# Two token tiles, one after the other in the last two weight chunks: a two-block transformer kernel on one core

## What is computed

```python
def second_block(x, ...):
    for layer in range(DEPTH):                       # two layers
        if layer % 2 == 0:
            y = even_mixer(x, ...)                   # its last product is ev_out
        else:
            y = odd_mixer(x, ...)                    # its last product is od_out
        x = layer_norm(ALPHA * x + y, ln1_g[layer], ln1_b[layer])
        f = conv_ffn(x, ...)                         # fup0/fup1 up, fdown0/fdown1 down
        x = layer_norm(ALPHA * x + f, ln2_g[layer], ln2_b[layer])
    return x

def layer_norm(x, g, b):
    mu = x.mean(-1, keepdims=True)
    var = jnp.square(x - mu).mean(-1, keepdims=True)
    return (x - mu) * lax.rsqrt(var + LN_EPS) * g + b
```

## Time and profile before

| | us |
|---|---|
| median of three runs | 1284.06 |
| the three runs | 1279.86, 1292.66, 1284.06 |
| span of the profiled execution | 1289.9 |

### The profile page before, as it was taken

How to read it: one execution, slowest core, us unless ns; L and a number is a source line. 1 busy time by engine, 2 the same in 40 slices (tenths; PEclk the granted TensorE clock), 3 DMA queues, 4 the chain that set the end, 5 groups by cost and what they waited for, 6 DMA issues and landing times.

```text
span 1289.9 us, 22283 instructions
## 1 busy us (share of the span) xinstructions
PE 1226.5 (95%) x8846; PEld 1143.1 (89%) x8846; DVE 536.4 (42%) x948; ACT 671.7 (52%) x920; POOL 957.2 (74%) x750
## 2 busy tenths in 40 slices
PE   4899999999989999999999998999998898999997
PEld 4788999999968999999987778999887776999985
DVE  4866331110485242110543745744204646464502
ACT  5366555443665555343544346666536555565541
POOL 5856679979843879889695346998895844898893
PEclk9799999999989999999999798999998998999999
DMA  6563345554431445545553124464453432555451
GB/s 260 196 181 103 131 160 208 189 187 169 173 121 38 163 160 200 195 162 196 196 176 126 66 96 157 173 229 170 180 205 131 164 131 99 180 212 195 168 193 33
DMA packets 33140, 208.69 MB, mean 162 GB/s; under 512 B 3432, under 2 KB 7656, under 8 KB 8472
## 3 DMA queue, kind: packets, MB, share of 16 engines
q1 hardware_dynamic: 29728, 199.22, 43.1%
q10 hardware_dynamic: 3320, 8.14, 2.0%
HBM read 206.29 MB, written 1.59 MB: 161 GB/s over the span
## 4 chain that ended last, share of the span: by engine, by line
POOL 55%; issue 24%; PE 17%; DVE 2%; ACT 1%; DMA 0%; POOLq 0%; DVEq 0%; SPq 0%; ACTq 0%
POOL w_lo L2317 55%; PE bank L284 5%; PE bank L286 5%; PE bank L285 5%; ACT w_hi L1069 0%; DMA raw<-stream 0%; DVE stats L1658 0%; ACT arena L1505 0%; PE bank L1011 0%; ACT h L1167 0%; DVE bank L1672 0%; POOLq L2314 0%; PE bank L1026 0%; DVE arena L2257 0%; DVE stats L1666 0%
## 5 line engine op out<-in xcount | busy, mean ns | idle before, releaser
L2317 POOL TENSOR_TENSOR w_lo<-raw,w_hi 128x512 fp32r<-128x512 f32 x744 | 954.4, 1322 | 312.5 <-ACT w_hi L1069 312.2
L284 PE MATMUL bank<-xs_hi,w_hi 128*128 128x256 f32 x1648 | 477.6, 290 | 23.7 <-POOL w_lo L2317 17.3
L285 PE MATMUL bank<-xs_lo,w_hi 128*128 128x256 f32 x1648 | 473.6, 287 | 0.0
L286 PE MATMUL bank<-xs_hi,w_lo 128*128 128x256 f32 x1648 | 473.3, 287 | 0.0
L1069 ACT ACTIVATE w_hi<-raw 128x2048 fp32r<-128x2048 f32 x186 | 354.5, 1913 | 194.5 <-PE bank L286 159.4
L284 PEld LDWEIGHTS bank<-xs_hi,w_hi 128*128 128x128 f32 x1648 | 324.1, 197 | 30.6 <-issue 30.0
L285 PEld LDWEIGHTS bank<-xs_lo,w_hi 128*128 128x128 f32 x1648 | 324.2, 197 | 0.4 <-issue 0.2
L286 PEld LDWEIGHTS bank<-xs_hi,w_lo 128*128 128x128 f32 x1648 | 323.9, 197 | 0.0
L284 PE MATMUL bank<-hT_hi,w_hi 128*128 128x256 f32 x680 | 194.6, 286 | 2.1 <-issue 1.9
L286 PE MATMUL bank<-hT_hi,w_lo 128*128 128x256 f32 x680 | 192.3, 283 | 0.0
L285 PE MATMUL bank<-hT_lo,w_hi 128*128 128x256 f32 x512 | 144.9, 283 | 0.0
(11 more groups left out here) (312 smaller groups left out, 1409.2 us busy)
## 6 DMA issues: line engine op xcount, KB each, us to landing
raw<-stream SPq DMA_DIRECT2D x186, 1024.0 KB, 4.8
arena<-ln_rows ACTq DMA_DIRECT2D x4, 1024.0 KB, 5.7
arena<-vec_scratch ACTq DMA_DIRECT2D x8, 256.0 KB, 8.7
con<-consts SPq DMA_DIRECT2D x1, 1288.0 KB
h<-x SPq DMA_DIRECT2D x1, 1024.0 KB, 4.9
out<-h SPq DMA_DIRECT2D x4, 256.0 KB, 2.4
con<-pool_mat ACTq DMA_DIRECT2D x1, 768.0 KB, 8.4
vec_scratch<-vec_row ACTq DMA_DIRECT2D x1, 512.0 KB
```

The source lines that it names most:

```text
L284: mm(out, lh, rh, start=start, stop=False, skip_group_check=True)
L285: mm(out, lh, rl, start=False, stop=False, skip_group_check=True)
L286: return mm(out, ll, rh, start=False, stop=stop, skip_group_check=True)
L2317: ins = nc.gpsimd.tensor_tensor(w_lo[:, slot_c].rearrange("p a b -> p (a b)")[:, part], raw[:, slot_r, part], w_hi[:, slot_c].rearrange("p ...
```

## The change

The last two chunks ahead of each norm are used for token tile 0 first and for tile 1 after it. In last_half, chunk c is used for both tiles with k = 0 and 1, for tile 0 with k = 2 and 3, and its last two steps, tile 1 with k = 2 and 3, come behind tile 0's steps of chunk c + 1. In down_by_tokens both last chunks are waited for, then tile 0 takes all eight steps, then tile 1. used_up for the first of the two chunks moves with its last step. VectorE's piece(0, 1) moves behind invert(0) for i = 5 and 7. No operation is added or taken away.

```diff
--- before.py
+++ after.py
@@ -345,19 +345,23 @@
                 c = START[name] + 2
                 hi, lo = half_views(c)
                 o = [claim(pe, (name, 1, t)) for t in range(TT)]
-                for k in range(4):
-                    pe.wait_ge(S("xs_ready"), XS[wait] - 3 + k)
-                    for t in range(TT):
-                        last = by_tokens(o[t], hi, lo, k, src, k, t, start=(k == 0), stop=(k == 3))
-                used_up(last)
+                steps = [(0, 0), (0, 1), (1, 0), (1, 1), (2, 0), (3, 0)]
+                for k, t in steps:
+                    if t == 0:
+                        pe.wait_ge(S("xs_ready"), XS[wait] - 3 + k)
+                    last = by_tokens(o[t], hi, lo, k, src, k, t, start=(k == 0), stop=(k == 3))
+                filled(last, (name, 1, 0))
+                sums()
+                hi2, lo2 = half_views(c + 1)
                 for t in range(TT):
-                    filled_by_chunk((name, 1, t), c)
-                sums()
-                hi, lo = half_views(c + 1)
-                for t in range(TT):
-                    o = claim(pe, (name, 1, 2 + t))
+                    if t == 1:
+                        for k in (2, 3):
+                            last = by_tokens(o[1], hi, lo, k, src, k, 1, start=False, stop=(k == 3))
+                        used_up(last)
+                        filled_by_chunk((name, 1, 1), c)
+                    o2 = claim(pe, (name, 1, 2 + t))
                     for k in range(4):
-                        last = by_tokens(o, hi, lo, k, src, k, t, start=(k == 0), stop=(k == 3))
+                        last = by_tokens(o2, hi2, lo2, k, src, k, t, start=(k == 0), stop=(k == 3))
                     if t == 0:
                         filled(last, (name, 1, 2))
                 used_up(last)
@@ -386,21 +390,34 @@
             def down_by_tokens(name, kt, ready, i):
 
                 chunks, o = 2 * kt // 4, {}
-                for c in range(chunks):
+
+                def step(c, hi, lo, u, t):
+
+                    n, k = divmod(4 * c + u, kt)
+                    key = (name, 2 * n + t)
+                    if n == 0 and t == 0:
+                        pe.wait_ge(S("hidden_ready"), ready + k + 1)
+                    if k == 0:
+                        o[n, t] = claim(pe, key)
+                    last = by_tokens(o[n, t], hi, lo, u, (hT_hi, hT_lo), k, t, start=(k == 0), stop=(k == kt - 1))
+                    if k == kt - 1 and (n, t) != (1, 1):
+                        filled(last, key)
+                    return last
+
+                for c in range(chunks - 2):
                     hi, lo = half_views(START[name] + c)
-                    steps = [(u, t) for u in range(4) for t in range(TT)] if c < chunks - 1 else \
-                        [(u, t) for t in range(TT) for u in range(4)]
-                    for u, t in steps:
-                        n, k = divmod(4 * c + u, kt)
-                        key = (name, 2 * n + t)
-                        if n == 0 and t == 0:
-                            pe.wait_ge(S("hidden_ready"), ready + k + 1)
-                        if k == 0:
-                            o[n, t] = claim(pe, key)
-                        last = by_tokens(o[n, t], hi, lo, u, (hT_hi, hT_lo), k, t, start=(k == 0), stop=(k == kt - 1))
-                        if k == kt - 1 and (n, t) != (1, 1):
-                            filled(last, key)
+                    for u in range(4):
+                        for t in range(TT):
+                            last = step(c, hi, lo, u, t)
                     used_up(last)
+                final = {c: tuple(half_views(START[name] + c)) for c in (chunks - 2, chunks - 1)}
+                for t in range(TT):
+                    for c in final:
+                        hi, lo = final[c]
+                        for u in range(4):
+                            last = step(c, hi, lo, u, t)
+                        if t == 1:
+                            used_up(last)
                 filled_by_chunk((name, 3), START[name] + chunks - 1)
                 if i < 8:
                     turned(i)
@@ -1678,7 +1695,8 @@
                         .then_inc(S("result_dve"), 1)
 
                 piece(0, 0)
-                piece(0, 1)
+                if i in (6, 8):
+                    piece(0, 1)
                 piece(1, 0)
                 if i == 8:
                     dve.wait_ge(S("ln_rows_loaded"), 16 * 4)
@@ -1695,6 +1713,8 @@
                     finished(0, 1)
                     return
                 invert(0)
+                if i in (5, 7):
+                    piece(0, 1)
                 piece(1, 1)
                 invert(1)
                 key = last_piece(i, 1, 1)
```

## The result

| | before | changed |
|---|---|---|
| median of 20 runs each | 1281.31 us | 1286.95 us |
| lowest, highest | 1274.74, 1292.66 | 1281.44, 1295.25 |
| span of the profiled execution | 1289.9 | 1283.9 |
| last matmul ahead of norm 5 to the end of the span | 510.0 | 516.5 |

The ratio changed to before is 1.0054, 95% interval 1.0033 to 1.0074: the change makes the kernel 0.5% slower, 6.9 us (4.2 to 9.5), or 5.6 by the medians. So I compare from the last matmul ahead of norm 5 to the end: 1289.9 - 779.89 = 510.0 and 1283.9 - 767.41 = 516.5.

The account below looks back on a forecast made before the run. TensorE, busy 95% of the span, bounds the long stages; serial chains bound the norms' ends. 2.63 + 1.48 + 0.93 - 0.80 = +4.2 us on the 1284.06 median gave 1288.3 us, range 1280 to 1297.

Parts of the forecast that it names:

- the queue: ScalarE runs in order: its last cut, released 2.72 us later, stands ahead of the norm's table warm-up, square roots and normalisations.
- Norm 5, +2.63: Layer norm after ev_out: tile 1's square root starts 2.63 us later, at 784.88 against 782.25; bounds 2.3 and 3.9.
- Norm 6, +1.48: Layer norm after fdown0: second square root 1.48 us later, from 977.68 to 979.16; bounds 1.05 and 2.7.
- Norm 7, +0.93: Layer norm after od_out: second root 0.93 us later, with the last matmul 0.67 later; bounds 0.4 and 2.2.
- Norm 8, -0.80: Layer norm at the end, no cut left: piece(1, 1) starts 0.80 us earlier; bounds 0 and -0.9.
- The holds: At norms 5, 6 and 7, L1666, with two SBUF inputs, is held to the end of a GpSimd operation.
- rival C: L1666 falls between GpSimd operations at each norm and the restart catches higher clock earlier: 1.0 us slower, 1285; chance 0.14.
- E: Every hold goes the bad way and the clock adds 2: 10.0 us slower, 1294; chance 0.07.
- Rival D: fdown0 and fdown1: TensorE stops, waiting for two chunks at once, up to 5.4 us each; say 1295; chance 0.05.
- Rival B: Tile 0's lead arrives because ScalarE's cut isn't in the way: 3.1 us faster, 1281.0; chance 0.12.
- The table load: Norms 5 and 6: no drain after the load; the skill's 1.4 us drain each would make the sum near 7.
- the clock: TensorE's low granted clock after norms: longer idle could change it by 1.5 us each; taken as nothing, 2 either way.

Follow-up runs that it names:

- e4: The kernel before with only the new last_half, and VectorE's new order in norms 5 and 7 alone; ratio to before 1.0041.
- e9: e1 with tile 1's k = 2 step of od_out moved back ahead of tile 0's k = 3; ratio to the kernel before 0.9989.
- e1: The changed kernel with ScalarE's last cut ahead of norms 5, 6 and 7 put behind the norm; ratio to the kernel before 0.9954.
- e10: e9 with seven idle matmuls of 256 columns added to each of norms 5, 6 and 7; ratio to the kernel before 0.9941.
- e2: The kernel before, old tile order, with ScalarE's last cut put behind the norm; ratio to before 0.9953.
- e8: The changed kernel run and traced once more, unaltered; ratio to the kernel before 1.0072.
- e11: The kernel before run and traced once more, unaltered; ratio 1.0011.
- e3: The kernel before with only the new down_by_tokens (norms 6 and 8), VectorE's order left as it was; ratio to before 1.0006.
- e5: The changed kernel with the square-root table loaded ahead of ScalarE's last cut, the cut still ahead of the norm; ratio to before 1.0038.
- e12: The kernel before with the cut behind the norm, five idle matmuls a norm and the new order in fdown1 alone; ratio to before 0.9932.

## Why the prediction was right, and where it was short

The forecast was 4.2 us slower, for the reason of the queue; measured are 5.6 by the medians and 6.9 by the ratio, whose interval goes from 4.2 to 9.5. That the median itself, 1286.95, lies only 1.35 below the forecast's 1288.3 is luck in part: the median of three runs from which the forecast started was 2.75 above that of twenty, and the change was taken 1.4 too low.

- Norm 5, +2.63: the second root moved from 2.36 to 4.95 us behind the last matmul's end, +2.59. The cut, the table load, the hold of L1666 and the two pieces stood where the working had them. That piece(0, 1) was moved behind the inversion is a part of it, as forecast: tile 0's bank was long there.
- Norm 6, +1.48: the root moved by 1.43 (2.37 to 3.80), the gap by 1.86. The rest, 0.4, is tile 1's transposes at the low clock (1.97 us against 1.15), as in e4; the prediction let them be as fast as before.
- Norm 7, +0.93: 0.27 in the root, plus the hole ahead of it, worked out at 0.67; e9, which fills that hole, measured 0.71.
- Norm 8, -0.80: the tail is 0.87 shorter.
- The holds: L1666 was to end 1.91, 1.91 and 0.62 us behind the last matmul's end of norms 5, 6 and 7, and ended 1.88, 1.88 and 0.65 behind it, each time with the end of one GpSimd operation. Neither rival C, which has it fall between two operations, nor E, which has it wait for one end more, came about.
- The cover taken for the sweep and for the two chunks held: no wait of TensorE for GpSimd appeared at either place. Rival D is out. Rival B, a gain if the queue weren't there, was priced at 3.1 us; e1's rest is 3.0 to 3.8 us below the two traces of before, and its timed ratio is lower still.
- The table load: load and activation follow each other with 0.02 us between them (766.72 + 1.28, then 768.02). By the rule of the Trainium skill, page ScalarE: Activation LUTs, section What ACT_TABLE_LOAD costs, a drain of 1.4 us would lie there. It doesn't here, and the sum of 7 that the rule gave rested on a wait that no row has.
- The term that was short, as far as the runs show it, is the clock, "I take nothing, and 2 us either way". It has a direction. The windows of the gaps and of the 10 us behind them, changed kernel and then the kernel before (columns as in e10, the granted clock third from the end):

```profile
767.41:777.26 9.85, 3.71 (x17) 2.40 (x17) 7.65 (x17) 6.74 (x16) 4.33 (x4) 0.72 0.34 127
777.26:787.26 10.00, 9.99 (x66) 10.00 (x67) 2.72 (x5) 5.31 (x8) 5.03 (x4) 0.77 0.04 7
966.13:974.83 8.70, 3.91 (x16) 2.59 (x17) 6.26 (x15) 6.63 (x16) 4.31 (x4) 0.70 0.43 157
974.83:984.83 10.00, 10.00 (x65) 10.00 (x66) 2.77 (x6) 7.44 (x11) 5.02 (x4) 0.75 0.05 8
1077.57:1086.32 8.75, 3.60 (x17) 2.40 (x17) 7.61 (x16) 5.76 (x13) 4.32 (x4) 0.77 0.34 120
1086.32:1096.32 10.00, 10.00 (x61) 10.00 (x62) 2.10 (x4) 4.76 (x8) 5.01 (x4) 0.69 0.00 1
```

```profile
779.89:787.15 7.26, 3.61 (x16) 2.40 (x17) 5.88 (x14) 5.65 (x13) 1.65 (x2) 0.74 0.51 178
787.15:797.15 10.00, 10.00 (x72) 10.00 (x73) 3.38 (x6) 6.01 (x8) 5.05 (x4) 0.85 0.05 8
975.31:982.16 6.85, 2.79 (x16) 1.67 (x17) 5.77 (x14) 5.70 (x13) 1.64 (x2) 0.94 0.55 207
982.16:992.16 10.00, 10.00 (x61) 10.00 (x62) 2.71 (x5) 7.26 (x11) 5.03 (x4) 0.70 0.06 8
1083.06:1091.54 8.48, 3.61 (x17) 2.40 (x17) 6.95 (x15) 5.81 (x14) 1.63 (x2) 0.74 0.34 124
1091.54:1101.54 10.00, 10.00 (x62) 10.00 (x63) 2.24 (x4) 4.90 (x8) 5.03 (x4) 0.71 0.00 1
```

Low clock is 2 x (1 - clock) x length. For norm 6 of the changed kernel that is 2 x 0.30 x 8.70 + 2 x 0.25 x 10 = 10.2 us; before, 2 x 0.06 x 6.85 + 2 x 0.30 x 10 = 6.8. Over the three norms the record of the granted clock has 30.7 us in both traces of the changed kernel and 23.9 in both of before. In all traces without idle matmuls it has 36 such gaps: of 17 longer than 8.3 us, 15 went with a low period of 10.2 us; of 19 shorter ones, one did, the others with 6.8 or 3.4. (I drew that line afterwards, between the gaps of 7.85 and 8.32; no run looked for a limit.) At norm 7 it was 10.2 in both kernels; what the change lengthened is at norms 5 and 6. Most of the longer period falls into the gap itself, where only the transposes feel it: 0.4 us in norm 6, nothing in norm 5, where they were slow before as well. That is the part of the excess over 4.2 that is shown.

The other 1.0 us of the traces' 5.6 isn't. By the means of two traces each, the stretch behind norm 5 is 0.2 shorter in the changed kernel, that behind norm 6 1.4 longer (0.7 of it from the hole), that behind norm 7 0.6 longer. The low clock in the 10 us behind the restarts is 0.9 us more in the changed kernel (15.8 and 14.0 against 14.9 and 13.2), which costs half of that. But the two traces of before differ by 1.3, 0.5 and 0.9 us in these three stretches themselves, so this may be spread.

What stays open is the timed ratios' own spread: against their traces, e1 and e2 came out some 2 us faster, e9 2 us and e8 4 us slower.

## What to carry to other kernels

An engine's program is a queue. A release that comes later costs whatever stands behind the instruction that waits for it, so when a buffer's last use is moved, look for the prefetch that waits for it and ask what latency-bound work is behind it; here the fix was to put that prefetch behind the norm, and it was worth 0.5%, in the old order too. A tiny vector operation on the critical chain should have one tensor in SBUF and not two, where GpSimd's sweep runs beside it. And look at the granted clock in and behind a gap of TensorE: here the gaps cost again there, and idle matmuls that fitted into TensorE's waits took that away (another 5 us).

## What the hardware showed that I had not expected

- A VectorE operation on one column of 128 values, 0.16 us alone, took up to 1.28 us beside GpSimd (e11 and e3, norm 7), always to the end of one of its 128x512 operations; with one SBUF tensor and a column scalar it took 0.21 and was never held, in six norms.
- The hold can move: with the chain 1.4 us earlier (e5) the second inversion fell into the sweep and took 1.22.
- Seven idle float32 matmuls of 256 columns in each gap (6.2 to 6.9 us, e10), or five (6.2 to 6.9 us, e12), kept the granted clock at 1.00 in all three norms; in e9, without them, it was at the low level, 1.2 GHz, for 6.8 us at each. The Trainium skill, page TensorE: Matmul & The Clock Gate, section HAM oscillation — how this bites in real kernels, tells of a kernel in which each wait for the next tile brings TensorE back to the slow level, so that the tile starts slow; the runs here agree in the direction.
